# q projected in pairs of tiles with seven block products, k and v projected from x directly behind the gate, and the norms of q and k taken in channels

## What is computed

```python
def hybrid_layer(x, ...):
    h = rms_norm(x, norm_g)
    proj = h @ w_in            # q k v | z_a | p | z_b | u v_sgu | z_c | glu_a glu_b | z_d | merge
    q = apply_rope(rms_norm(q.reshape(B, S, N_Q_HEADS, HEAD_DIM), q_norm_g), cos, sin)
    k = apply_rope(rms_norm(k.reshape(B, S, N_KV_HEADS, HEAD_DIM), k_norm_g), cos, sin)
    o_a = window_attention(q, k, v, attn_sinks)
    o_b = multiscale_pool(p_in, pool_mix, pool_scale)
    o_c = spatial_gating(u, v_sgu, sgu_ln_g, sgu_ln_b, sgu_w, sgu_b)
    o_d = conformer_conv(glu_a, glu_b, conv_w, conv_b, conv_ln_g, conv_ln_b)
    ...                        # each times silu(z), times w_branch, times sigmoid(merge), summed
    return x + mixed @ w_out
```

## Time and profile before

| | |
|---|---|
| median of 3 runs (2059.39 to 2060.28 us) | 2059.4 us |
| profiled execution, first to last instruction | 2057.5 us |
| the runs' median less that span | 1.9 us |
| TensorE busy | 2049.7 us |
| GpSimd busy | 1259.9 us |
| VectorE busy | 1366.5 us |
| ScalarE busy | 882.2 us |
| granted clock of TensorE | 1.000 |

### The profile page before, as it was taken

The page is one execution under the profiler, slowest core; times in us unless marked ns, Lnnn a source line. Parts: engine busy times, 40 slices in busy tenths (PEclk is TensorE's granted clock), DMA queues, the critical chain, the costliest instruction groups (busy, mean ns, idle before and its releaser), DMA issues.

```text
span 2057.5 us, 27183 instructions
## 1 busy us (share of the span) xinstructions
PE 2049.7 (100%) x9680; PEld 1700.8 (83%) x9680; DVE 1366.5 (66%) x1629; ACT 882.2 (43%) x1659; POOL 1259.9 (61%) x950
## 2 busy tenths in 40 slices
PE   9999999999999999999999999999999999999999
PEld 8898877888888888888888888878888888888887
DVE  5896544788878645338769964438888786453484
ACT  6624664343233334324655256543432343443242
POOL 3367444776769667554723664447766697675545
PEclk9999999999999999999999999999999999999999
DMA  7103232313431343413421122233134213434132
GB/s 277 52 32 103 88 103 98 95 60 74 94 75 52 83 82 75 141 52 117 144 89 47 42 98 97 87 104 97 52 83 96 65 52 82 92 72 143 42 133 103
DMA packets 108006, 183.63 MB, mean 89 GB/s; under 512 B 13664, under 2 KB 23136, under 8 KB 107872
## 3 DMA queue, kind: packets, MB, share of 16 engines
q1 hardware_dynamic: 88656, 151.13, 22.9%
q0 software_dynamic: 9216, 16.78, 5.9%
q10 hardware_dynamic: 10000, 13.98, 1.9%
HBM read 139.90 MB, written 41.95 MB: 88 GB/s over the span
## 4 chain that ended last, share of the span: by engine, by line
PE 96%; DVE 2%; ACT 1%; DVEq 0%; issue 0%; DMA 0%; SPq 0%; ACTq 0%
PE acc L725 81%; PE aux L794 6%; PE acc L794 4%; DVE flo L1531 1%; PE aux L869 1%; PE aux L888 1%; PE aux L879 1%; PE aux L903 1%; PE aux L831 0%; PE acc L831 0%; PE aux L845 0%; ACT fhi L995 0%; DVEq L1795 0%; DVE csum_lo L1531 0%; DMA allp<-cols 0%
## 5 line engine op out<-in xcount | busy, mean ns | idle before, releaser
L656 POOL TENSOR_TENSOR wlo<-raw,whi 128x512 fp32r<-128x512 f32 x392 | 550.6, 1406 | 491.8 <-ACT whi L995 490.8
L725 PE MATMUL acc<-fhi,whi 128*128 128x512 f32 x2024 | 793.3, 392 | 2.0 <-DVE v L1528 2.0
L725 PE MATMUL acc<-fhi,wlo 128*128 128x512 f32 x2024 | 788.9, 390 | 0.0
L725 PE MATMUL acc<-flo,whi 128*128 128x512 f32 x2024 | 788.6, 390 | 0.0
L725 PEld LDWEIGHTS acc<-fhi,whi 128*128 128x128 f32 x2024 | 380.1, 188 | 83.5 <-issue 4.3
L725 PEld LDWEIGHTS acc<-fhi,wlo 128*128 128x128 f32 x2024 | 380.1, 188 | 79.3
L725 PEld LDWEIGHTS acc<-flo,whi 128*128 128x128 f32 x2024 | 380.3, 188 | 77.2
L656 POOL TENSOR_TENSOR wlo<-wsum,whi 128x512 fp32r<-128x512 f32 x210 | 299.1, 1424 | 210.3 <-ACT whi L995 209.6
L995 ACT ACTIVATE whi<-raw 128x512 fp32r<-128x512 f32 x392 | 245.2, 626 | 385.0 <-PE acc L725 331.1
L1535 DVE SCALAR_TENSOR_TENSOR aux<-conv,allp,aux 128x1024 f32<-128x1024 f32 x232 | 299.0, 1289 | 20.4 <-issue 0.9
L995 ACT ACTIVATE whi<-wsum 128x512 fp32r<-128x512 f32 x210 | 131.9, 628 | 203.8 <-PE acc L725 159.9
(11 more groups left out here) (210 smaller groups left out, 2486.3 us busy)
## 6 DMA issues: line engine op xcount, KB each, us to landing
raw<-wstream SPq DMA_DIRECT2D x392, 256.0 KB, 2.7
md<-prev POOLq DMA_DIRECT2D x64, 256.0 KB, 4.2
x<-x SPq DMA_DIRECT2D x32, 256.0 KB, 5.0
md<-prev SPq DMA_DIRECT2D x32, 256.0 KB, 3.6
out<-x ACTq DMA_DIRECT2D x32, 256.0 KB, 2.1
mx<-md SPq DMA_DIRECT2D x24, 256.0 KB, 5.1
xrow<-x_rows SPq DMA_DIRECT2D x8, 512.0 KB, 6.8
qd<-qst ACTq DMA_DIRECT2D x16, 256.0 KB, 2.2
```

The source lines that it names most:

```text
L656: nc.gpsimd.tensor_tensor(wlo[:, f % SLOTS, :], src, whi[:, f % SLOTS, :].bitcast(F32), ALU.subtract).then_inc(lo_made, 1)
L725: mm = nc.tensor.matmul(dst, w, m[:, kt0 + k, cols], start=first and k == 0 and n == 0, stop=last and k == UK - 1 and n == 2, skip_group_c ...
```

## The change

* **Order.** `PLAIN` becomes VS, KV, and Q becomes the first stage of `STAGES`: two pairs, (Q, 0) and (Q, 1), before U.
* **KV** multiplies x without its norm, like VS, and `take_kv` multiplies the result by 1/rms for each token as ACT copies it out, to `krow` and `vt`. `h_rounded`, `h_rest` and `h_all` go. `X_SLOT` moves, so that x lies in the slots F6, F5, F7 and B21, and the forms of h go to them as KV leaves them (`form_rounded` waits for KV's steps).
* **q** comes out with channels on partitions, low halves of four heads in one tile (`qlo`) and high halves in the other (`qhi`). `turn_q` with its copies goes; `turn_k` stays and moves to (Q, 0). The sums of squares over a head are made by TensorE with matrices of ones (`head_sums`, three of them: k, and each pair of q), in two fp32r parts. The root is exp(-ln/2) on ACT (`inverse_root`).
* **Rotation** is done by DVE in channels: `rotate_k` after (Q, 1)'s p3, `rotate_q` of pair 0 in U's first pair (first turn, `sum_x`, first join, `sum_v`, `sum_22`, a product, second turn, a product, `sum_12`, a product, second join), of pair 1 around ZC's first pair. `sgu_mix` of groups 2 and 3 waits for the last of pair 0's rotation, since both use `aux`. The table loads (`load_rope`, 2 x 512 KB), the exchange of k's halves (`swap_k`, 4 DMAs) and the stores of q (`store_q`, 8 DMAs for each pair) are issued by ACT. `load_q` becomes two DMAs with rows of 64 elements.
* **sgu_mix** moves to (Q, 1) and (U, 1) and uses the banks `aux` for all four groups.
* In O's last pair, `x_rounded` of the next layer's first four tiles runs after p5 in place of p6.

```diff
-PLAIN = (("VS", 8), ("Q", 8), ("KV", 4))
-STAGES = (("U", 2), ("ZC", 2), ...
+PLAIN = (("VS", 8), ("KV", 4))
+STAGES = (("Q", 2), ("U", 2), ("ZC", 2), ...
...
-                token_major(L, "VS", 8)
-                token_major(L, "Q", 8)
-                token_major(L, "KV", 4, {0: lambda L=L: row_sums(L), 2: lambda L=L: sgu_mix(L, (0, 1))})
-                pe.wait_ge(sgu_taken, 4 * L + 2)
-                pair(L, "U", 0, {"p7": lambda L=L: sgu_mix(L, (2, 3))})
-                pair(L, "U", 1, {"p2": lambda L=L: (pe.wait_ge(ident_loaded, 16), turn_q(L, 0)),
-                                  "p4": lambda L=L: turn_q(L, 1)})
-                pair(L, "ZC", 0, {"p6": lambda L=L: turn_q(L, 2), "p2": lambda L=L: turn_q(L, 3)})
-                pair(L, "ZC", 1, {"p1": lambda L=L: turn_k(L)})
+                token_major(L)
+                keys_values(L)
+                pair(L, "Q", 0, {"p3": lambda L=L: turn_k(L), "p4": lambda L=L: row_sums(L)})
+                pair(L, "Q", 1, {"p1": lambda L=L: sgu_mix(L, (0, 1)), "p7": lambda L=L: head_sums(L, 0),
+                                 "p4": lambda L=L: head_sums(L, 1)})
+                pair(L, "U", 0)
+                pair(L, "U", 1, {"p6": lambda L=L: sgu_mix(L, (2, 3)), "p4": lambda L=L: head_sums(L, 2)})
+                for i in range(2):
+                    pair(L, "ZC", i)
...
+            def head_sums(L, n):
+                pe.wait_ge(qk_low, 3 * L + n + 1)
+                pe.wait_ge(sgu_taken, 4 * L + n + 1)
+                block_ones = bones_r if n else heads_r
+                for t in range(2):
+                    at = slice(t * HALF, (t + 1) * HALF)
+                    nc.tensor.matmul(aux[:, n % 2, at], block_ones[:], sqh[n][:, at], start=True, stop=False)
+                    mm = nc.tensor.matmul(aux[:, n % 2, at], block_ones[:], tmp_r[n][:, at], start=False, stop=True)
...
+                plain_pair("Q", 0, first_of(qlo[0]), {
+                    "p1": lambda: take_kv(L, 1), "p6": sgu_scales,
+                    "p5": lambda: form_rounded(L, ("F4", 0), ("F4", 1)),
+                    "p7": lambda: normal_vs(L, 0, range(TT)),
+                    "p3": lambda: (take_turned_k(L), square_a(L, 0), square_high(L, 0))})
+                plain_pair("Q", 1, first_of(qlo[1]), {
+                    "p1": lambda: square_a(L, 1),
+                    "p6": lambda: (square_b(L, 1), load_rope(L)), "p5": lambda: normal_vs(L, 1, range(4)),
+                    "p7": lambda: (square_high(L, 1), swap_k(L), inverse_root(L, 0)),
+                    "p2": lambda: normal_vs(L, 1, range(4, TT)), "p3": lambda: inverse_root(L, 1)})
...
+            def inverse_root(L, n):
+                nc.scalar.activation(aux[:, n % 2, :], aux[:, n % 2, :], ACT.Ln, bias=epst[:], scale=1.0 / HD)
+                nc.scalar.activation(aux[:, n % 2, :], aux[:, n % 2, :], ACT.Exp, scale=-0.5)
...
+            def rotate_k(L):
+                scaled(kraw[:], kraw[:], allp[:, L, C_KA:C_KA + 1], cost[:], ALU.mult)
+                scaled(kt[:], kt[:], allp[:, L, C_KB:C_KB + 1], sint[:], ALU.mult)
+                add(kt[:], kt[:], kraw[:])
+                mul(kt[:], kt[:], aux[:, 0, :])
+            def rotate_q(L, i):
+                a_, b_, both, root = qlo[i], qhi[i], aux[:, i, :], aux[:, 1 - i, :]
+                def turn(t):
+                    scaled(both[:, 0:HALF], a_[:, at], allp[:, L, C_QL:C_QL + 1], sint[:, at], ALU.mult)
+                    scaled(both[:, HALF:SEQ], b_[:, at], allp[:, L, C_QH:C_QH + 1], sint[:, at], ALU.mult)
+                    scaled(a_[:, at], a_[:, at], allp[:, L, C_QL:C_QL + 1], cost[:, at], ALU.mult)
+                    scaled(b_[:, at], b_[:, at], allp[:, L, C_QH:C_QH + 1], cost[:, at], ALU.mult)
+                def join(t):
+                    sub(a_[:, at], a_[:, at], both[:, HALF:SEQ])
+                    add(b_[:, at], b_[:, at], both[:, 0:HALF])
+                    mul(a_[:, at], a_[:, at], root[:, at])
+                    mul(b_[:, at], b_[:, at], root[:, at])
+                return lambda: turn(0), lambda: join(0), lambda: turn(1), lambda: join(1)
...
+                form(L, "F4")
+                sum_x(L, "Q", 0)
+                form_rest(L, ("F4", 0), ("F4", 1))
...
+                scaled(shift[:], mv[:, :, 0], -1.0, rstd[:, 1, :], ALU.mult).then_inc(vs_scales, 1)
+                sum_v(L, "Q", 0)
...
+                sum_12(L, "Q", 1, qlo[1][:, HALF:SEQ]).then_inc(taken["c"], 1)
+                rotate_k(L)
+                sum_21(L, "Q", 1, qhi[1][:, 0:HALF]).then_inc(taken["d"], 1)
+                turns = rotate_q(L, 0)
+...
-                               {"p6": lambda i=i: next_rounded(i, "p6", (0, 1)),
-                                "p5": lambda i=i: next_rounded(i, "p6", (2, 3))})
+                               {"p5": lambda i=i: next_rounded(i, "p5", (0, 1, 2, 3))})
```

More of the change, by code:

```diff
@@ L717, in _, with three @@
         def _(pe):
-            def three(dst, hi, lo, slot, kt0, first, last, cols=slice(0, HALF), resumed=False):
+            def three(dst, hi, lo, slot, kt0, first, last, cols=slice(0, HALF), resumed=False, half=None):
                 for k in range(UK):
+                    if half and k == UK // 2:
+                        half()
                     wh = whi[:, slot, k * P:(k + 1) * P]
@@ L797, in token_major @@
-                        if n_tile == 3 and k == n - 1 and name != "KV":
+                        slot = (L * FORMS + FORM["VS", kx]) % SLOTS
+                        s = X_SLOT[kx // UK, tile // 4]
+                        at = slice(tile % 4 * P, (tile % 4 + 1) * P)
+                        for m, (h, w) in enumerate(((fhi, whi), (flo, whi), (fhi, wlo))):
+                            mm = nc.tensor.matmul(tile_bank(tile), h[s][:, kx % UK, at], w[:, slot, :],
+                                                  start=kx == 0 and m == 0, stop=kx == KT - 1 and m == 2)
@@ L1200, in square_k, with normal_vs @@
[L1200 to L1204 removed]
+            def normal_vs(L, e, tiles):
                 act.wait_ge(vs_scales, L + 1)
                 for t in tiles:
[L1207 to L1209 removed]
@@ new lines, in take_kv @@
+            def take_kv(L, c):
+                act.wait_ge(rms_turned, 16 * (L + 1))
+                act.wait_ge(step_done, stepped(L, "KV", 3))
+                for t in range(TT):
+                    nc.scalar.activation((krow, vt)[c][:, t, :], kv_bank(t)[:, c * P:(c + 1) * P], ACT.Copy,
+                                         scale=rms[:, t:t + 1]).then_inc(kv_taken, 1)
+            def take_turned_k(L):
+                act.wait_ge(turned, L + 1)
+                copy(kraw[:], aux[:, 0, :]).then_inc(k_copied, 1)
@@ new lines, in square_b, with square_high @@
+            def square_b(L, n):
+                st, i = QK_AT[n]
+                act.wait_ge(taken["d"], bank_n(L, "d", (st, i), 2))
+                act.wait_ge(row_summed, L + 1)
+                if n == 2:
+                    act.wait_ge(qk_summed, 3 * L + 2)
+                nc.scalar.activation(sqs[:], QK_B[n][:], ACT.Square).then_inc(qk_squared, 1)
+            def square_high(L, n):
+                if n:
+                    act.wait_ge(qk_added, 2 * L + n)
+                else:
+                    act.wait_ge(qk_squared, 5 * L + 1)
+                copy(sqh[n][:], tmp[n][:]).then_inc(qk_high, 1)
@@ L1651, in rotate, with form @@
-            def rotate(L, n):
-                for step in rotate_steps(L, n):
-                    step()
+            def form(L, q):
+                for n in range(2):
+                    at = slice(2 * n, 2 * n + 2)
+                    b11, b12, b22, b21 = (b[:, at, :] for b in (x11, x12, x22, x21))
+                    dve.drain()
+                    if q == "F5":
+                        op = sub(b11, b11, b12)
+                    elif q == "F7":
+                        op = sub(b12, b22, b12)
+                    elif q == "F6":
+                        op = scaled(b22, b22, -1.0, b11, ALU.subtract)
+                    else:
+                        op = scaled(b21, b22, -1.0, b21, ALU.subtract)
+                    op.then_inc(form_made, 1)
@@ L1989, in _ @@
                     mul(b_[:, 0:HALF], b_[:, 0:HALF], BANK_AP["d"]).then_inc(taken["d"], 1)
-                    if i == 0:
-                        last_mixes()
-                    else:
-                        rotate(L, 4)
-                        rotate(L, 5)
-                dve.drain()
-                for i in range(2):
-                    gate_pair(L, "ZC", i, branch_c)
+                dve.drain()
+                turns = rotate_q(L, 1)
+                turns[0]()
+                gate_pair(L, "ZC", 0, branch_c, 0, 0, {"x": turns[1], "11": turns[2]})
+                turns[3]()
+                gate_pair(L, "ZC", 1, branch_c)
                 for i in range(4):
```

669 lines of the change are left out of this document (309 added, 360 removed).

## The result

The changed kernel takes 2098.1 us (median of 4 runs, 2097.4 to 2098.5) against 2059.5 for the kernel before on the same chip: 1.0186 times as long, 95% interval 1.0171 to 1.0200. It is 38.6 us slower, where 5.0 were forecast. The profiled execution has a span of 2096.7 us and a time of 2098.5.

A forecast was written before the change was run, and what follows sets the result against it. TensorE's step count bounds the kernel (busy 2049.7 of 2057.5 us). Waits of 3.0 + 5.2 + 0.5 = 8.7 us a layer against 6.2 gained add 5.0 in all: 2064.4 us, 8-in-10 range 2049 to 2071.

The forecast's parts named there:

- PE's steps: TensorE's matmul count: Q gains 5.41 us, `turn_q` 3.49, `head_sums` costs 2.72; 6.2 us a layer gained.
- The term of 12.4: The gain in TensorE's steps over both layers, 6.2 us a layer.
- The forms of h in layer 1: Before (Q, 0)'s p5: h's forms ready at 76, needed at 79.1, margin 3 us; wait taken as 0.
- The first wait: Before (Q, 0)'s p3, TensorE waits for `sum_v` to free bank c: 3.0 us a layer, from 0.8 to 3.5.
- Count from KV's end. ACT's queue: ...: Step of the wait before (Q, 0)'s p3: ScalarE's queue takes 10.3 us, F4's first copy ends at 11.4.
- In layer 2 ... the margin is over 12 us: Forms of h in layer 2: h begins at 1048.4, KV ends near 1098.6, so no wait.
- each counts in full: Pricing of U's waits: everything on TensorE stands behind them, so each adds its full length.
- The second wait: In U, DVE's list from `rotate_k` to pair 0's last join holds TensorE: 5.2 us a layer, bounds 0 and 8.
- my middle between the two: U's wait taken as 5.2: between 6.8 (POOL delays 11 instructions) and 3.6 (only 7 that write to SBUF).
- Ln and Exp lie in different table sets: Rival: three `inverse_root` hold five more loads of 1.28; some 4 us more a layer, 2072; chance 0.09.
- The third wait: Before `scores` in MC, q's way through DRAM: 0.5 us a layer, from 0 to 2.5.
- ACT issues the stores between two `high`s, which then come up to 4 us late and have about that in hand: Step of the term for q's way through DRAM, which was taken as 0.5 us a layer.

The follow-up runs named there:

- e13: Changed kernel with statistics behind `v`, pair 1's stores on SP, U's rotation reordered, roots sharing table loads, U1's mix later: 2055.1 us, 0.9977 of the kernel before.
- e7: Changed kernel with B22 rounded early and the gate's statistics, with what hangs on them, moved behind `v`: 2082.6 us, 15.5 less than the changed kernel.
- e3: Changed kernel with ScalarE rounding h's block B22 ahead of its eight copies out of the VS banks: 2094.3 us, 3.8 less.
- e4: Changed kernel with 24 extra matmuls, whose result nobody reads, in the wait before (Q, 0)'s p3: 2096.0 us, 2.1 less.
- e1: Changed kernel with both activations of the inverse root (Ln, Exp) made copies, so no table loads for it: 2089.9 us, 8.2 less.
- e12: Changed kernel with k and pair 0 sharing table loads and DVE waiting for k's root only before k's last product: 2090.8 us, 7.3 less.
- e5: Changed kernel with the eight stores of q's pair 1 issued by SyncE ahead of q's reload, instead of by ScalarE: 2088.6 us, 9.5 less.

## Why the prediction was wrong

**PE's steps: right.** KV took 51.36 to 74.39, 23.0 us as counted, and `turn_k` and the groups of four in `head_sums` their 0.87 and 0.91. In e13, 129.2 us lie between KV's end and the first scores in layer 1. Six pairs of 19.05, `turn_k`, two mixes, `row_sums` and three `head_sums` are 125.5, and 2.6 are waits; 1.1 are left over. The term of 12.4 is good to the 3.8 us above.

**The forms of h in layer 1: right.** I had 39 us from 36.7, ready at 76; the rests of F6 and F5 ended at 76.2. p6 and p7 waited 0.3 and 0.8.

**The first wait: wrong, 3.0 against 8.6 and 7.2.** The step that failed is "Count from KV's end. ACT's queue: ...". I took ScalarE's list as what holds F4's first copy, ending 11.4 us behind KV (the items of that queue add up to 10.5 and not 10.3, which changes nothing). It ended 17.2 behind, since ScalarE itself stood 4.0 us for DVE's `mv`. The sum that I should have made is DVE's own, from F5's rests on to `v`: eight more statistics, four rests for F7 and B21, the aggregation, F4's form, F4's rests. The prices of all but the small instructions stood in the earlier trace rows; the trace has 23.0 us from 76.2, ending at 99.2, 24.8 behind KV and not 17.5. I had summed that list up to F5 and dropped it there. e7, which takes the statistics and what hangs on them out of its middle, won 15.5 us, with e3's 3.8 among them.

**"In layer 2 ... the margin is over 12 us": wrong in size.** KV ended at 1120.1 and the rests of F6 and F5 at 1118.8, so before p5 the margin was under 7 us, as KV's end lay 1.2 us behind the rests and two block products follow it. That was enough for p5 and p7, which did not wait, but the early start of h did not reach `v`: B22's rounding stands behind copies that wait for VS (e3), F6's behind KV. The wait before p3 was 7.2 against 8.6 in layer 1.

**Idle time was priced at its length: wrong.** "each counts in full" is too little. e4 showed that the granted clock is what slows the steps behind a wait: 14 matmuls at 0.43 us after 8.6 us of idle time, 8 after 3.2. That is 10.5 us over the run, over a quarter of the loss, for which the prediction's sum has no term. No row of the kernel before could show it, since TensorE never stood there for over 1.1 us.

**The second wait: right in size, and partly for another reason.** 5.2 us a layer were forecast. Layer 1 has 6.0, at the three places named (1.73, 2.94, 1.30). Layer 2 has 4.6 (1.68, 2.94): there TensorE ran at half clock from 1201.1 to 1204.5 and came to the mix later than DVE's last join. VectorE's first rotation of pair 0:

```profile
139.40 0.76 DVE L1583 SCALAR_TENSOR_TENSOR aux<-qlo,allp,sint 128x512 f32<-128x512 f32 x1 [0.39 <-ACT aux L1304]
140.06 1.79 DVE L1583 SCALAR_TENSOR_TENSOR aux<-qhi,allp,sint 128x512 f32<-128x512 f32 x1
141.93 1.61 DVE L1583 SCALAR_TENSOR_TENSOR qlo<-qlo,allp,cost 128x512 f32<-128x512 f32 x1
```

The first of them has POOL beside it for 0.25 us only, the others all the time. Beside POOL, instructions with two operands in SBUF take 1.6 to 1.8 us, and those that write to PSUM (`aux`) as long as the others. By this the recorded count gives a wait of 6.8. The Trainium skill (GPSIMD Engine Reference, Specifications) names two SBUF inputs as what contends, and makes no exception for what is written; the trace agrees, and my middle between the two had nothing for it. But e1 and e12 show that about half of the wait came from the late roots: with the same rotation, what is left in U is one wait for `v`, 2.2 and 3.1 us. That 5.2 lies between 4.6 and 6.0 is therefore in part luck: the prediction had the late roots in a rival and not in its sum.

**The rival "Ln and Exp lie in different table sets": true, at 0.09.** I priced it at 4 us a layer, and e1 measured 4.1. The Trainium skill (ScalarE: Activation LUTs, Table sets: the hidden batching unit) has one set for both functions; here twelve loads of 1.283 us stand at six roots, so the trace does not agree, and the measurement decides. I had let the rule push the rival down with nothing of the trace behind it.

**The third wait: wrong, 0.5 against 3.2, and in another place.** The reload was on time: `scores` started 0.3 us late in layer 1 and 0.1 in layer 2, and q's reload landed in 2.8 as before with its rows of 256 bytes. The step that failed is "ACT issues the stores between two `high`s, which then come up to 4 us late and have about that in hand". The `high`s had it. The gate's silu in the same list did not, and DVE's list hung on it (e5, 9.5 us for both layers with the clock).

**The sum.** Forecast were 8.7 us of waits a layer. Found: 8.6 and 7.2 in the first stretch with 1.1 of small ones in layer 1, 6.6 and 5.2 in U with the small ones for weights, 3.3 a layer in MC, and some 5 a layer of half clock. Of the 33.6 us that the forecast was short, about 11 are the first wait's size, 10.5 the clock, 6 MC's wait, 1.5 U's, 2 what the waits cost beyond their entries, and some 3 are what I can't place.
